# A two-block transformer kernel on one core: four small moves in the hand-written order of VectorE and TensorE work

## The reference, cut to what matters

```python
h = x
for i in range(2):
    mix = gla_mixer(h, ...) if i == 0 else mlstm_mixer(h, ...)
    h = layer_norm(ALPHA * h + mix, ln_g[i, 0], ln_b[i, 0])
    ffn = grouped_moe(h, router_w, moe_w1[i], moe_w3[i], moe_w2[i])   # 2 of 16 experts for each token
    h = layer_norm(ALPHA * h + ffn, ln_g[i, 1], ln_b[i, 1])
# second block, for l in range(2):
ada = silu(c) @ w_ada[l] + b_ada[l]      # 1024 x 6144, one row of 6144 numbers
```

## Time and profile before

| | us |
|---|---|
| median of 3 runs (lowest, highest) | 1627.64 (1624.3, 1631.57) |
| the profiled execution | 1624.3 |
| its span, first to last instruction | 1622.4 |
| PE busy | 1564.7 (96%) |
| DVE busy | 897.9 (55%) |
| ACT busy | 646.6 (40%) |

### The profile page before, as it was taken

The page is one execution under the profiler, slowest core; times in us unless marked ns, Lnnn a source line. Parts: engine busy times, 40 slices in busy tenths (PEclk is TensorE's granted clock), DMA queues, the critical chain, the costliest instruction groups (busy, mean ns, idle before and its releaser), DMA issues.

```text
span 1622.4 us, 21016 instructions
## 1 busy us (share of the span) xinstructions
PE 1564.7 (96%) x8552; PEld 1077.1 (66%) x8552; DVE 897.9 (55%) x1372; ACT 646.6 (40%) x1050; POOL 41.6 (3%) x67
## 2 busy tenths in 40 slices
PE   8999999997999989999989999999999999999998
PEld 7775444433887743444357775798897777678997
DVE  4786021214897731121179864677777975666555
ACT  5352111112644411111156764534446766444443
POOL 0100000000000000000030000000002000000000
PEclk9999999999999999999999999999999999999999
DMA  9967999999664589999955444576783454547541
GB/s 313 322 225 291 390 424 420 423 423 277 206 167 169 205 359 413 429 426 422 414 189 179 156 168 176 198 276 248 259 304 115 153 208 148 190 155 278 190 156 26
DMA packets 115565, 425.35 MB, mean 262 GB/s; under 512 B 5052, under 2 KB 7576, under 8 KB 102536
## 3 DMA queue, kind: packets, MB, share of 16 engines
q1 hardware_dynamic: 111808, 416.81, 68.1%
q0 software_dynamic: 2304, 6.95, 1.5%
q10 hardware_dynamic: 1352, 0.18, 0.1%
HBM read 421.82 MB, written 1.05 MB: 261 GB/s over the span
## 4 chain that ended last, share of the span: by engine, by line
PE 77%; DVE 10%; ACT 5%; DVEq 4%; issue 2%; DMA 1%; ACTq 0%; SPq 0%
PE bank L626 37%; PE bank L1465 14%; PE bank L1483 7%; PE bank L1450 4%; PE bank L1495 3%; PE bank L2721 2%; DVE ring_r L2982 2%; DVEq L727 2%; DVE parts_dit L577 1%; ACT parts_dit L574 1%; DVE ada_part L728 1%; DMA ring<-in_w_ff 1%; PE bank L2723 1%; PE bank L749 1%; PE bank L814 1%
## 5 line engine op out<-in xcount | busy, mean ns | idle before, releaser
L1465 PE MATMUL bank<-ring,arena 128*64 128x512 f32 x1024 | 226.1, 594 | 1.5 <-ACT arena L1561 1.5
L1750 DVE TENSOR_TENSOR arena<-arena,bank 128x512 f32<-128x512 f32 x16 | 16.7, 1044 | 363.0 <-PE bank L1465 363.0
L626 PE MATMUL bank<-ring_r,x_hi 128*128 128x512 f32 x528 | 210.0, 398 | 0.0
L577 DVE TENSOR_TENSOR parts_dit<-ring,parts_dit 128x2048 fp32r<-128x2048 f32 x66 | 151.2, 2291 | 80.7 <-ACT parts_dit L574 80.6
L1465 PEld LDWEIGHTS bank<-ring,arena 128*64 128x64 f32 x1024 | 72.7, 137 | 139.7 <-issue 139.7
L574 ACT CAST parts_dit<-ring 128x2048 fp32r<-128x2048 f32 x66 | 125.0, 1896 | 95.7 <-PE bank L626 95.7
L626 PE MATMUL bank<-parts_dit,f_hi 128*128 128x512 f32 x512 | 160.6, 395 | 2.6 <-DVE parts_dit L577 1.9
L626 PE MATMUL bank<-x_hi,parts_dit 128*128 128x256 f32 x896 | 162.9, 280 | 0.1
L626 PEld LDWEIGHTS bank<-x_hi,parts_dit 128*128 128x128 f32 x896 | 138.4, 188 | 2.1 <-DVE parts_dit L577 1.8
L626 PE MATMUL bank<-in_whi,x_hi 128*128 128x512 f32 x304 | 125.5, 413 | 0.8 <-DVE x_lo L2423 0.8
L1483 PE MATMUL bank<-arena 128*64 128x512 f32 x512 | 115.1, 603 | 10.8 <-ACT arena L1587 10.8
(11 more groups left out here) (374 smaller groups left out, 2569.8 us busy)
## 6 DMA issues: line engine op xcount, KB each, us to landing
ring<-in_moe_w SPq DMA_DIRECT2D x64, 2048.0 KB, 12.6
ring<-in_w_ff SPq DMA_DIRECT2D x32, 2048.0 KB, 8.9
arena<-in_moe_w SPq DMA_DIRECT2D x28, 2048.0 KB, 13.3
ring<-in_w_ada SPq DMA_DIRECT2D x24, 2048.0 KB, 8.8
ring<-in_w_in SPq DMA_DIRECT2D x20, 2048.0 KB, 8.2
ring<-in_mlstm_w_in SPq DMA_DIRECT2D x8, 2048.0 KB, 15.8
ring<-in_gla_w_in SPq DMA_DIRECT2D x5, 2048.0 KB, 13.3
arena<-in_moe_w SPq DMA_DIRECT2D x8, 1024.0 KB, 10.4
```

Of the source, the lines that this page charges most:

```text
L577: return nc.vector.tensor_tensor(part_view(where, 1, h, form), half_of(ring[:, SLOT_OF[n], :], form, h), part_view(where, 0, h, form).bitc ...
L626: last = pe.matmul(out, a[ka], b[kb], start=(first and i == 0), stop=(final and i == 2))
L1465: last = pe.matmul(bank[halves[h], :], s_x[:, p % 2, c, halves[h]], w[h][:, c, :], start=(c == 0), stop=(c == DC - 1))
```

## The change

Four edits, in three stages:

1. GLA stage, DVE: the ada steps of chunk 3 were four at step 21 and four at the end of step 22's extra work. They become three at 21 and five at 23.
2. MoE stage, PE: the unused matmuls at the end of the dense path in layer 0 are 8, before 24.
3. mLSTM stage, DVE: the last three ada steps of chunk 8 go from step 26 to step 25.
4. Start of the mLSTM stage, DVE: the first of the three weight splits goes ahead of the four `x_lo`.

```diff
         GLA_WORK = {8: (1, 0, 1), 9: (1, 1, 5), 10: (1, 5, 6), 11: (1, 6, 8), 14: (2, 0, 2), 15: (2, 2, 3), 16: (2, 3, 7),
-                    17: (2, 7, 8), 21: (3, 0, 4)}
-        GLA_LAST = (3, 4, 8)
+                    17: (2, 7, 8), 21: (3, 0, 3), 23: (3, 3, 8)}
...
                 if n == 22:
                     for i, b in enumerate(HALVES[0]):
                         turned_lo(dve, 1, i, b, 6 + i)
-                    mixer_ada(dve, GLA_LAST)
...
             if l == 0:
-                keep_clock(pe, ps[0], 24)
+                keep_clock(pe, ps[0], 8)
...
-                   20: (8, 0, 2), 21: (8, 2, 3), 24: (8, 3, 5), 26: (8, 5, 8)}
+                   20: (8, 0, 2), 21: (8, 2, 3), 24: (8, 3, 5), 25: (8, 5, 8)}
...
+            mix_weight_lo(dve, base, *ML_STEPS[0], "cols")
             for b in range(4):
                 turned_lo(dve, 3, b, b, 4 + b)
-            for n in range(LOOK):
+            for n in range(1, LOOK):
                 mix_weight_lo(dve, base + n, *ML_STEPS[n], "cols")
```

## The result

The changed kernel takes 1638.38 us (median of 5 runs, 1636.02 to 1640.3) against 1629.39 us for the kernel before: ratio 1.0059, 95% interval 1.0044 to 1.0076. A second group of six runs gave 1.0064 (1.0043 to 1.0084). So it is slower, by 0.6%: nine to ten microseconds where I had forecast 5.4 and called it no change. 1638.38 lies inside the stated range, but close to its end. The profiled execution took 1636.92 us, with a span of 1635.1 us, 12.7 more than before (of which some is chance: the profiled execution of the kernel before was the fastest of its five runs).

The account below looks back on a forecast made before the run. PE was taken to bound the kernel, busy for 96% of the span. The terms 3.4 + 1.7 + 0.3 + 0 = 5.4 us, added to the median of 1627.64, gave 1633 us (0.33% slower), range 1626.5 to 1639.

Parts of the forecast that it names:

- What bounds the kernel, and which MoE path ran: Whole kernel: PE bounds it, busy for 96% of the span; the MoE stage ran the gathered path, not the dense one.
- Edit 1, the wait: GLA stage: PE waits 2.9 us, then 0.4 us, for late gated(1) tiles before the second turn: +3.4 us.
- the clock falls behind a new stall: Rival: PE's clock drops behind the new GLA or mLSTM wait; 1634.7 us for one fall, 1636.4 for two; chance 0.25.
- Edit 2: mLSTM stage: earlier ada steps delay head 2's state update, so PE waits: +1.7 us, no gain from earlier weight loads.
- Edit 3: Start of the mLSTM stage: the split ahead of the x_lo delays PE's gate matmuls: +0.3 us, bounds 0 and 1.2.
- Edit 4: Dense path of layer 0: the cut matmuls do not run; the jump changes by 0 to 1.9 us either way; sum 0.
- The sum is the same at both ends: Layer 0 jump: a shorter one gains nothing because DVE sets the gate matmuls' start; only a longer one shows, up to 2.8 us.
- Its lower bound: Range's low end, 1626.5 us: 1633 less 2.8 us (GLA stall at its lower bound, both mLSTM edits repaid) and 3.7 us of spread.
- slower by over 0.5%: Outcome of a measured time above 1635.8 us: chance 0.22, against 0.75 for within 0.5%.
- the absorbed stall: Rival: the stalls vanish in the MoE stage or are repaid by a shorter jump; 1628 to 1631 us; chance 0.17.
- the dense path: Rival: the 16 cut matmuls do run in the timed runs, giving back 18.9 us; 1614 us; chance 0.02.
- the queue: Rival: the first MoE pair's weights come 5.5 us later and PE waits for them; 1638.5 us; chance 0.05.

Follow-up runs that it names:

- e10_hole: Kernel before with one ada step of chunk 3 moved from step 21 to the end of step 22, five ahead of the split: ratio 0.9990.
- after_again: The changed kernel, all four edits, run again unaltered for a second group of six runs: ratio 1.0064 to the kernel before.
- e8_gla_fill: Kernel before with only the GLA edit, two unused matmul calls in PE's new wait and two fewer in the dense path: ratio 1.0029.
- e1_gla: Kernel before with only the GLA edit (ada steps of chunk 3: three at 21, five at 23): ratio 1.0035.
- e5_edits123: The changed kernel with the 24 unused matmuls of the dense path put back: ratio 1.0058 to the kernel before.
- kc56: Kernel before with 56 unused matmul calls in the dense path instead of 24: a single execution, 1629.91 us.

## Why the prediction was wrong

**What bounds the kernel, and which MoE path ran**: right. No row of the dense path appears.

**Edit 1, the wait**: right in each step. The hole 3.54 us wide (3.5 forecast), the five steps 4.05 us (4.0), `gated(1)` at 116.24 (116.05, in a trace that ran 0.17 us later), PE's gap 3.01 us (2.9), the second turn 3.3 us late (3.4). e10_hole shows that it is this wait and not DVE's extra work. The late load of ada chunk 4 (issued at 116.17) cost nothing: after_again has the MoE stage of layer 0 at the same length as before.

**Edit 1, the clock**: this is the step that failed. I had it as the rival "the clock falls behind a new stall", at 1.7 us for one place, with a chance of 0.25, and left it out of the sum, so that this term stood at nothing. The clock fell behind the gap in all four profiled kernels that have it unfilled, in one of the three that have it filled, and in none of the nine without it. From the second turn to the end of the 48 matmuls the four took 3.5, 1.9, 3.5 and 4.3 us more than the kernel before (the changed kernel, after_again, e1_gla, e5_edits123; 0.4 of each is the wait between the two token tiles, which e8_gla_fill has without a fall). That is mostly more than 1.7, because a fall lasted up to twice or three times as long as the one that I had read the price from (about 3 us at the lower clock in after_again, 7 in the changed kernel and e1_gla, 10 in e5_edits123). Up to the first gather it was 3.5, 1.9, 5.7 and 6.4 us, but the last two hold the second fall, which kc56 has without a gap. The timed runs of edit 1 alone leave 2.4 us (by the ratio) to 3.7 us (on the means) beside the wait of 3.3. Reading 3.33 us of idle with a fall and 3.3 us of expected idle as "near that length, but shorter" was the error: the new gap was of the size of the only row that I had, and that row showed a fall.

**Edit 2**: right. 1.69 us of waiting (1.7 forecast), the granted clock at 1.00 behind it in every profile that has the wait, 2.0 us timed, and the earlier weight load pays nothing.

**Edit 3**: right within what can be told. 0.3 forecast, 0.5 timed, interval around zero.

**Edit 4**: right in the sum, wrong in a part. The unused calls take no time, and the jump did not get shorter with the path. "The sum is the same at both ends" overlooked that moving the target can also put a stall behind it: a gap of 0.9 to 2.3 us in the gate matmuls in three of the five profiles with 8 or 72 calls, never with 24, and one of 0.35 us further on with 56. Why the timed runs show no cost of it (0.9991, and e5_edits123 as slow as the changed kernel) is left open. What the profiles do show is that the gate matmuls run at the lower clock in six kernels without the gap too, and then take 3.5 to 3.6 us instead of 1.9, so that not all of the 5.6 us in the changed kernel is the gap's. A shorter jump may be another part: with the target moved it took 6.5 to 9.7 us, with 24 calls 8.5 to 9.9. But the shortest of all, 5.97 us, is that of e8_gla_fill, where the target has not moved.
By the Trainium skill ("Runtime: NRT & Kernel Launch", Instruction fetch mechanics) instructions arrive in blocks of 256 and are loaded ahead only in sequence. The equal place of the gap with 8 and with 72 calls, 256 instructions apart, agrees with it, and so does the gap with 56 calls, 64 instructions further on.

**The sum and the chances**: the waits of 5.4 us came as forecast, each within half a microsecond; what was missing is the clock, about 5 us by the estimate from all runs. The two make 10.4 us, about one more than the 9.3 to 9.7 measured, which is within the noise of the estimate. That the time lay inside the range is due to two falls of the clock and a longer jump in its upper bound, not to the sum. (Its lower bound has a slip: the stall at 3.0 and edits 2 and 3 repaid is 2.4 us less, not 2.8.) With a term for the clock, "slower by over 0.5%" would have been the likeliest case rather than one of 0.22. The rivals of the absorbed stall, the dense path and the queue did not happen: the MoE stage passed the delay on in full (239.2 us from its first gather to the jump in the kernel before, 239.1 in after_again).

## What to carry to other kernels

Filler work on an engine that is not the bound belongs in its holes, and what matters is not how late it ends but what is queued behind it: the same five instructions cost nothing ahead of a split that waited anyway, and 6 to 7 us behind it. Where a new wait on TensorE comes near the length of one behind which the trace shows a lower clock, put the price of a fall into the sum, not into a rival, and take it from several falls, since they differ in length. The mean granted clock of all runs tells the clock's share better than one profile, where a fall can also stand that has nothing to do with the edit. Short waits that are already there can be worth filling with matmuls that nobody reads: one call in a gap of 1.26 us made this kernel 0.22% faster and steadier.

## What I had not expected of the hardware

- A fall of the clock behind a gap of 3.01 us did not last equally long: the 48 matmuls behind it took 12.88 to 14.14 us in the four profiles with the gap unfilled, 11.36 to 11.38 without a fall. Single runs of the kernel before spread over 10 us, and those of the kernel with the filled MoE gaps over 3.4.
- A jump of PE over a path that is not run took 6.0 to 9.9 us in layer 0, 9.65 and 6.53 us in two executions of the same kernel, and its length did not follow that of the path (7.07 us with 72 calls, 9.25 with 56).
- With 56 calls in the path, PE stood still for 0.35 us at 64 instructions behind the place of the gap with 8 calls.
